# Moving the later SBUF buffers of a two-block transformer kernel up by 32 bytes, and one zero matmul more in nine groups of matmuls

## The chip, the cores and the metric

The kernel runs on one core of a Trainium2 chip, as one launch. The metric is the device time of that launch in microseconds (us). Below, TensorE is PE, its weight loads are PEld, VectorE is DVE, ScalarE is ACT, GpSimd is POOL, and SyncE is SP, which issues the loads of the weights.

## What is computed

Two transformer blocks of depth 1 run one after the other on x of 256 tokens by 2048 features, in float32. Each block is modulated by a vector c through one large matrix-vector product (`w_mod`, `w_ada_2`, 2048 to 12288).

```python
def first_block(x, c, ...):
    mod = (silu(c) @ w_mod + b_mod)                     # six vectors of 2048
    h = rmsnorm(x, mix_pre_w) * (1 + sc_m) + sh_m
    y = hybrid_mixer(h, w_in, ..., w_out)               # short convolution beside gated linear attention
    x = x + g_m * rmsnorm(y, mix_post_w)
    h = rmsnorm(x, ffn_pre_w) * (1 + sc_f) + sh_f
    y = conv_ffn(h, w_up, ffn_conv_w, w_down)           # 2048 -> 2 x 5632 -> 2048
    return x + g_f * rmsnorm(y, ffn_post_w)

def second_block(x, c, ...):
    mod = silu(c) @ w_ada + b_ada
    proj = (rms_norm(x, norm1_w) * (1 + scale1) + shift1) @ w_in
    u_pool, q, k, v, g_a, g_b = split(proj)
    y_a = multiscale_pool(u_pool, ...) @ w_a_up
    y_b = stick_breaking_attention(q, k, v) @ w_b_up
    x = x + gate1 * ((sigmoid(g_a) * y_a + sigmoid(g_b) * y_b) @ w_o)
    h2 = rms_norm(x, norm2_w) * (1 + scale2) + shift2
    return x + gate2 * (square(relu(h2 @ w_ff1)) @ w_ff2)
```

## The kernel before

Activations lie transposed: 128 features on the partitions, 256 tokens along the free dimension, 16 such tiles for 2048 features. To keep float32 precision, each number is split in two parts that TensorE takes: a rounded high part and the rest. `H`, `Y`, `FB`, `YAB`, `MG` and `FC` hold for each tile 512 columns, the high parts of 256 tokens and behind them their rests. A weight tile of 128 x 128 has its high part in `WH` and its rest in `WL`: ACT rounds `raw` into `WH`, DVE subtracts into `WL`.

A product of one weight tile with one activation tile is then, in `run_tile`, a **pair** of matmuls, one of 512 columns and one of 256:

```python
PE.matmul(bank(n)[:, :], wh, rhs, start=(kk == 0), stop=False)                # L585
return PE.matmul(bank(n)[:, T:2 * T], wl, rhs[:, 0:T], start=False, stop=ends) # L586
```

or, for jobs in `FOLDED`, three matmuls of 256 columns (L582 to L584). The moving operand is the activation tile, so it is read from `H` in the stages w_up, w_in_2 and w_ff1; from `FB` in w_down; from `YAB` in w_a_up_2 and w_b_up_2; from `MG` in w_o_2; from `FC` in w_ff2.

The order of work is written out by hand. `SLOTS` is a list of slots; a slot is mostly one load of weights, that is one job of 8 to 16 tiles (one output tile of 128 features). All engines walk it, each with its own lag, and semaphores tie them: PE waits for a weight unit (`s_lo`), for its bank to be emptied (`s_taken`), and in the first job of a group (`opens`) once per tile for the activation tile. The stages stand in this order: w_in with its sixteen parts, w_out, `AT_NORM1`, w_up and w_down in four groups (`FB`; the last group is folded), `AT_NORM2`, w_in_2, w_a_up_2, then two gates `ga` and `gb` from w_in_2 (`gb` alternates with w_b_up_2: 16 tiles from `H`, 8 from `YAB`), w_o_2, `AT_NORM3`, w_ff1 and w_ff2 in four groups (`FC`; the last two groups follow one another).

Here and there PE does other small products between the halves of a slot (`side`: gated linear attention, pooling, attention heads). At two places, `AT_NORM1 + 9` and `AT_NORM3 + 12`, it issues `beat`: a matmul of bf16 zeros, 512 columns, into `PS[1]` at a moment when it holds nothing (L621). `zeros` (L618) is the same for clearing.

SBUF tensors are laid out one behind the other in the order of the `sb` calls. `X`, `H`, `raw`, `WH`, `WL` and the constants come first, `eps` is the last of the constants, and behind it lie, one over another by stage, `raw2`, `Y`, `Q1` and so on, `FB`, `Y2`, `M`, `YAB`, `MG`, `FC`. As built, `H` is at byte 32896 of each partition (a multiple of 64) and `eps` at 152512. `raw2`, `Y`, `FB0`, `M` and `FC0` are at 152544, `YAB` at 168928, `FB1` at 175072, `FC1` at 185312, `MG` at 189408: each is 32 bytes past a multiple of 64. A tile of `H`, `FB`, `YAB`, `MG` or `FC` is 2048 bytes in each partition.

Of the kernel before, what the change touches and what calls it, by code (L numbers as in the profile page):

```python
# [109 lines left out]
LOADS, UNITS, UNITS_OF = [], [], []  # L110
# [57 lines left out]
SLOTS = [ls for ls in QKV]  # L168
# [9 lines left out]
AT_GB = len(SLOTS)  # L178
SLOTS += slots_of(L_GB) + [[]] * 2
SLOTS += slots_of(L_WO) + [[]]  # L180
AT_NORM3 = len(SLOTS)
# [75 lines left out]
MOD_COUNT = {STREAM[i][1:]: c + 1 for c, i in enumerate(MOD_ITEMS)}  # L257

SPLITS = [[] for _ in range(NSLOT)]
MODS_AT = [[] for _ in range(NSLOT)]
# [19 lines left out]
def build(nc, A, out):  # L282
    with ExitStack() as ctx:
        def sb(name, shape, dt=F32, on=ctx):
            return on.enter_context(nc.sbuf_tensor(name, shape, dt))

        def ps(name, shape):
            return ctx.enter_context(nc.psum_tensor(name, shape, F32))

        def sem(name):  # L290
            return ctx.enter_context(nc.semaphore(name))

        V, S, PE, G, SP = nc.vector, nc.scalar, nc.tensor, nc.gpsimd, nc.sync
# [15 lines left out]
        rstd = sb("rstd", [128, T])  # L309
        rstd2 = sb("rstd2", [128, T])  # L310
        SX = sb("SX", [128, T])
        eps = sb("eps", [128, 8])

        PM = [ps(f"PM{i}", [128, 512]) for i in range(NBANK)]
        PS = [ps(f"PS{i}", [128, 1024]) for i in range(2)]
# [80 lines left out]
        def load_aps(l, slot):  # L396
# [47 lines left out]
        s_yc, s_yr, s_f, s_ya, s_yb, s_mg, s_f2 = (  # L444
            sem(x) for x in ("s_yc", "s_yr", "s_f", "s_ya", "s_yb", "s_mg", "s_f2"))
# [92 lines left out]
        def tensor():  # L538
# [49 lines left out]
            def run(ls, which):  # L588
                for t in range(len(UNITS[UNITS_OF[ls[0]][which]])):
                    for l in ls:  # L590
                        u = UNITS_OF[l][which]
                        if t == 0:
                            PE.wait_ge(s_lo, u + 1)
                        n, kk = UNITS[u][t]
                        m = RANK if JOBS[n].kind == "alr" else 128
                        c = slice(t * m, (t + 1) * m)
                        mm = run_tile(n, kk, WH[:, u % NUNIT, c], WL[:, u % NUNIT, c])
                        if t == len(UNITS[u]) - 1:
                            mm.then_inc(s_unit, 1)

            def run_v(l, which):

                u = UNITS_OF[l][which]
                k = UNITS[u][0][1]
                PE.wait_ge(s_lo, u + 1)
                for half in range(2):
                    hi = H[:, k, half * 128:half * 128 + 128]
                    lo = H[:, k, T + half * 128:T + half * 128 + 128]
                    for c in range(2):
                        b = slice(c * 512, (c + 1) * 512)  # L610
                        PE.matmul(PS[half][:, b], hi, WH[:, u % NUNIT, b], start=(k == 0), stop=False)  # L611
                        PE.matmul(PS[half][:, b], hi, WL[:, u % NUNIT, b], start=False, stop=False)  # L612
                        mm = PE.matmul(PS[half][:, b], lo, WH[:, u % NUNIT, b], start=False, stop=(k == 15))  # L613
                mm.then_inc(s_unit, 1)
# [5 lines left out]
            def beat(b):  # L620
                PE.matmul(b, zero.broadcast_to([128, 128]), zero.broadcast_to([128, 512]), start=True, stop=True)  # L621

            def clear(half, again):

                for c in range(2):
                    zeros(PS[half][:, c * 512:(c + 1) * 512])
                for _ in range(again):
                    zeros(PS[half][:, 512:1024], start=False)
# [17 lines left out]
            def y_sums(use):  # L646

                PE.wait_ge(s_yadd, 15 * (use + 1))
                PE.matmul(S0, mean[:, :], ST[use][:, 0, :], start=True, stop=False)
                PE.wait_ge(s_ysq, 16 * (use + 1))  # L650
                PE.matmul(S0, mean[:, :], SQ[use][:, 1, 0, :], start=False, stop=True).then_inc(s_ysum, 1)
                PE.matmul(S23, mean[:, :], ST[use][:, 1:3, :].rearrange("p q t -> p (q t)"), start=True, stop=False)
                PE.wait_ge(s_yz, 16 * (use + 1))
                PE.wait_ge(s_xz, 16 * (use + 1))
                PE.matmul(S23, mean[:, :], SQ[use][:, 1, 1:3, :].rearrange("p q t -> p (q t)"), start=False,
                          stop=True).then_inc(s_ysum, 1)

            def x_sums():
                PE.wait_ge(s_yadd, 45)
                PE.matmul(S0, mean[:, :], gt[:, 2, :], start=True, stop=False)  # L660
                PE.wait_ge(s_ysq, 48)
                PE.matmul(S0, mean[:, :], gt[:, 1, :], start=False, stop=True).then_inc(s_ysum, 1)
# [122 lines left out]
            def side(s, half):  # L785
                if AT_ALR <= s < AT_NORM1:
                    gla(2 * (s - AT_ALR + 7) + half)
                elif AT_NORM2 <= s < AT_GB:
                    heads(2 * (s - AT_NORM2 - 1) + half)

            start_up()
            for s, ls in enumerate(SLOTS):
                if s == AT_NORM1:
                    PE.wait_ge(s_gact, ACT_RSTD)
                    y_sums(0)
                    clear(1, 8)
                    PE.wait_ge(s_u, 1)
                    clear(0, 8)
                elif s == AT_NORM2:
                    PE.wait_ge(s_o, 2)  # L800
                    y_sums(1)
                    clear(1, 8)
                    PE.wait_ge(s_u, 2)
                    clear(0, 8)
                elif s == AT_NORM3:
                    PE.wait_ge(s_hdve, 11 + 6 * 3 + 2)
                    x_sums()
                    clear(1, 8)
                    PE.wait_ge(s_rstd, 6)
                    clear(0, 2)  # L810

                if s == AT_NORM1 + 9:
                    PE.wait_ge(s_o, 2)
                    beat(PS[1][:, 0:512])
                elif s == AT_NORM3 + 12:
                    PE.wait_ge(s_gh, 2)
                    for c in range(2):
                        beat(PS[1][:, c * 512:(c + 1) * 512])
                for n in DONE[s]:
                    if USE_OF[n]:  # L820
                        PE.wait_ge(s_taken[BANK_OF[n]], USE_OF[n])
                    else:
                        PE.wait_ge(s_at, BANK_OF[n] + 1)
                if s < AT_ALR:
                    for which in range(2):
                        run(ls[0:1], which)
                        run_v(ls[1], which)
                elif ls and ls[0] in L_V2:
                    if ls[0] == L_V2[0]:
                        PE.wait_ge(s_ya, 8)  # L830
                        PE.wait_ge(s_hact, 11)
                    run_v(ls[0], 0)
                    side(s, 0)
                    run_v(ls[0], 1)
                elif ls:
                    if ls[0] == L_AUP[0]:
                        PE.wait_ge(s_hact, 15)
                    run(ls, 0)
                    side(s, 0)
                    if len(UNITS_OF[ls[0]]) > 1:  # L840
                        run(ls, 1)
                side(s, 1)
# [913 lines left out]
        N_ALR = JOB_OF["alr", 0, 48]  # L1756

        tensor()
        scalar()
        vector()  # L1760
# [70 lines left out]
```

## Time and profile before

| | |
|---|---|
| time, median of 3 runs | 2525.01 us (2524.55 to 2526.55) |
| the profiled execution, its own time | 2522.16 us |
| its span | 2520.8 us |
| mean granted TensorE clock | 0.997 of full speed |
| PE busy / DVE busy / ACT busy | 2464.6 / 2001.0 / 1289.1 us |

The span is from the first to the last instruction. The profiled execution is one run, 2.85 us below the median of the three timed ones. Matmuls are pipelined and overlap in the record (a matmul of 512 columns is shown as 0.39 us long although the next starts 0.23 us later), so the pace of PE is read from the starts of successive matmuls and not from their durations.

### The profile page before, as it was taken

Reading aid. Unit: us, or ns where it says so; the run is one execution under the profiler, and the core shown is the slowest. Engines: PE = TensorE matmul, PEld = TensorE weight load, DVE = VectorE, ACT = ScalarE, POOL = GpSimd, SP = SyncE. Lnnn points to the kernel's source line nnn. Section 1 sums busy time; section 2 is a strip of 40 time slices with the busy share of each in tenths; the row PEclk is TensorE's granted clock in tenths of the full one; section 3 lists DMA queues with packets and bytes.
Section 4 is the critical chain, followed back from the end, with each engine's and each line's share of the span. In section 5 each row is a group of like instructions: output and inputs, shape, how many; then the busy total and the mean of one; then the engine's idle time right before and its main releaser. Section 6 shows DMA issues by size and latency. Waiting matters only on the chain.

```text
span 2520.8 us, 38361 instructions
## 1 busy us (share of the span) xinstructions
PE 2464.6 (98%) x15321; PEld 2203.0 (87%) x15321; DVE 2001.0 (79%) x2640; ACT 1289.1 (51%) x1883; POOL 4.0 (0%) x11
## 2 busy tenths in 40 slices
PE   6799999999999999999999999999999999999999
PEld 5689999898888888889888888888898888888888
DVE  7879998978977888889968688998678756556555
ACT  5454455555654555555546566554454444444443
POOL 0000000000000000000000000000000000000000
PEclk9999999999999999999999999999999999999999
DMA  9988898667777778778558677888578755555553
GB/s 374 391 306 315 327 356 298 238 223 271 266 256 263 259 250 291 260 258 267 180 190 331 232 281 261 321 316 293 184 259 316 259 184 189 194 185 188 193 188 134
DMA packets 142387, 652.16 MB, mean 259 GB/s; under 512 B 13009, under 2 KB 64209, under 8 KB 77441
## 3 DMA queue, kind: packets, MB, share of 16 engines
q1 hardware_dynamic: 141106, 645.06, 71.6%
q0 software_dynamic: 672, 3.31, 0.3%
q8 instruction: 121, 1.98, 0.3%
q10 hardware_dynamic: 432, 1.35, 0.2%
q14 instruction: 56, 0.46, 0.1%
HBM read 647.58 MB, written 2.10 MB: 258 GB/s over the span
## 4 chain that ended last, share of the span: by engine, by line
PE 82%; DVE 9%; DMA 4%; issue 2%; ACT 2%; DVEq 0%; SPq 0%; ACTq 0%
PE PM L585 45%; PE PM L586 23%; DVE WL L1224 3%; DVE raw L1231 3%; DMA raw<-in_w_in 3%; PE PM L582 2%; PE PM L583 2%; PE PM L584 2%; PE PS L582 2%; PE PS L583 2%; PE PS L584 2%; PE PS L611 1%; PE PS L612 1%; PE PS L613 1%; DMA raw<-in_w_mod 0%
## 5 line engine op out<-in xcount | busy, mean ns | idle before, releaser
L858 ACT CAST WH<-raw 128x1024 fp32r<-128x1024 f32 (+1 forms) x881 | 880.8, 1011 | 985.7 <-PE PM L586 658.7
L1224 DVE TENSOR_TENSOR WL<-raw,WH 128x1024 fp32r<-128x1024 f32 (+1 forms) x881 | 1016.6, 1172 | 419.0 <-ACT WH L858 416.4
L585 PE MATMUL PM<-H,WH 128*128 128x512 f32 x2944 | 1027.3, 393 | 0.0
L586 PE MATMUL PM<-H,WL 128*128 128x256 f32 x2944 | 823.1, 280 | 0.0
L585 PEld LDWEIGHTS PM<-H,WH 128*128 128x128 f32 x2944 | 551.3, 187 | 124.9 <-issue 0.4
L586 PEld LDWEIGHTS PM<-H,WL 128*128 128x128 f32 x2944 | 555.7, 189 | 0.1
L1231 DVE CUSTOM_DVE_ANT_0 raw<-raw,cb 128x2048 f32<-128x2048 f32 x192 | 437.0, 2284 | 1.7 <-DMA raw<-in_w_mod 1.2
L585 PE MATMUL PM<-FC,WH 128*128 128x512 f32 x1024 | 358.7, 393 | 0.0
L586 PE MATMUL PM<-FC,WL 128*128 128x256 f32 x1024 | 285.8, 279 | 0.0
L585 PEld LDWEIGHTS PM<-FC,WH 128*128 128x128 f32 x1024 | 191.9, 187 | 45.7
L582 PE MATMUL PM<-H,WH 128*128 128x256 f32 (+1 forms) x656 | 192.2, 293 | 35.7 <-DVE H L1255 29.8
L586 PEld LDWEIGHTS PM<-FC,WL 128*128 128x128 f32 x1024 | 191.9, 187 | 0.0
L584 PE MATMUL PM<-H,WL 128*128 128x256 f32 (+1 forms) x656 | 189.7, 289 | 0.0
L583 PE MATMUL PM<-H,WH 128*128 128x256 f32 (+1 forms) x656 | 189.6, 289 | 0.0
L585 PE MATMUL PM<-FB,WH 128*128 128x512 f32 x528 | 185.0, 393 | 0.0
L582 PEld LDWEIGHTS PM<-H,WH 128*128 128x128 f32 (+1 forms) x656 | 128.2, 195 | 43.0 <-DVE WL L1224 34.0
L586 PE MATMUL PM<-FB,WL 128*128 128x256 f32 x528 | 147.4, 279 | 0.0
L864 ACT COPY tmps<-PM 128x256 f32<-128x256 f32 x328 | 118.9, 363 | 54.1 <-PE PM L586 54.0
L583 PEld LDWEIGHTS PM<-H,WH 128*128 128x128 f32 (+1 forms) x656 | 128.3, 196 | 0.6
L584 PEld LDWEIGHTS PM<-H,WL 128*128 128x128 f32 (+1 forms) x656 | 128.4, 196 | 0.4
L585 PEld LDWEIGHTS PM<-FB,WH 128*128 128x128 f32 x528 | 98.9, 187 | 23.7
L582 PE MATMUL PS<-H,WH 128*128 128x256 f32 x384 | 108.9, 284 | 4.2 <-DVE H L1258 4.2
(329 smaller groups left out, 3125.2 us busy)
## 6 DMA issues: line engine op xcount, KB each, us to landing
raw<-in_w_ff SPq DMA_DIRECT2D x128, 1024.0 KB, 4.9
raw<-in_w_in SPq DMA_DIRECT2D x112, 1024.0 KB, 6.3
raw<-in_w_mod SPq DMA_DIRECT2D x96, 1024.0 KB, 7.1
raw<-in_w_ada SPq DMA_DIRECT2D x96, 1024.0 KB, 6.1
raw<-in_w_up SPq DMA_DIRECT2D x80, 1024.0 KB, 5.2
raw<-in_w_down SPq DMA_DIRECT2D x64, 704.0 KB, 5.2
raw<-in_w_out SPq DMA_DIRECT2D x16, 1024.0 KB, 6.6
raw<-in_w_o SPq DMA_DIRECT2D x16, 1024.0 KB, 6.2
```

Source lines behind the costliest of these rows:

```text
L582: PE.matmul(acc(n), wh, rhs[:, 0:T], start=(kk == 0 and not beside), stop=False)
L583: PE.matmul(acc(n), wh, rhs[:, T:2 * T], start=False, stop=False)
L584: return PE.matmul(acc(n), wl, rhs[:, 0:T], start=False, stop=ends)
L585: PE.matmul(bank(n)[:, :], wh, rhs, start=(kk == 0), stop=False)
L586: return PE.matmul(bank(n)[:, T:2 * T], wl, rhs[:, 0:T], start=False, stop=ends)
L611: PE.matmul(PS[half][:, b], hi, WH[:, u % NUNIT, b], start=(k == 0), stop=False)
L612: PE.matmul(PS[half][:, b], hi, WL[:, u % NUNIT, b], start=False, stop=False)
L613: mm = PE.matmul(PS[half][:, b], lo, WH[:, u % NUNIT, b], start=False, stop=(k == 15))
L858: S.copy(part(WH), w).then_inc(s_hi, 1)
L864: S.copy(low(n), bank(n)[:, T:2 * T]).then_inc(s_low, 1)
L1224: V.tensor_tensor(part(WL), w, part(WH).bitcast(F32), ALU.subtract).then_inc(s_lo, 1)
L1231: V.tensor_tensor_reduce(w, w, cb[:, :], 1.0, 0.0, ALU.mult, ALU.add, mods[:, which, tile:tile + 1]).then_inc(s_mod, 1)
```

## The change

`eps` gets 16 columns where it had 8, so that everything behind it lies 32 bytes higher: `raw2`, `Y`, `FB0`, `M` and `FC0` at 152576, `YAB` at 168960, `FB1` at 175104, `FC1` at 185344, `MG` at 189440, all multiples of 64. `ug`, `uv` and `exact` were at multiples of 64 and are now 32 bytes past one. And PE issues one more `beat` at the start of nine slots: the slot behind the first one of each group of w_down (four), of w_ff2 (four) and of w_o_2 (one).

```diff
+BEAT_AT = [s + 1 for s, ls in enumerate(SLOTS) if ls and LOADS[ls[0]][0] in ("w_down", "w_ff2_2", "w_o_2")
+           and LOADS[ls[0]][-1] == 0]
...
-        eps = sb("eps", [128, 8])
+        eps = sb("eps", [128, 16])
...
                 if s == AT_NORM1 + 9:
                     PE.wait_ge(s_o, 2)
                     beat(PS[1][:, 0:512])
                 elif s == AT_NORM3 + 12:
                     PE.wait_ge(s_gh, 2)
                     for c in range(2):
                         beat(PS[1][:, c * 512:(c + 1) * 512])
+                elif s in BEAT_AT:
+                    if AT_GB < s < AT_NORM3:
+                        PE.wait_ge(s_yb, 8)
+                    beat(PS[1][:, 0:512])
```

On PE, at the border between the first and the second job of the first group of w_ff2, stand before (FC0 is the moving operand, WH and WL the two parts of the weights, PM1 and PM2 the banks of the two jobs):

```order
L585 MATMUL PM1<-FC0,WH 128x512 [waits s_f2]
L586 MATMUL PM1<-FC0,WL 128x256
L585 MATMUL PM2<-FC0,WH 128x512 [waits s_lo,s_taken2]
L586 MATMUL PM2<-FC0,WL 128x256
L585 MATMUL PM2<-FC0,WH 128x512
```

and with the change (four lines were added above, so L585 is L589):

```order
L589 MATMUL PM1<-FC0,WH 128x512 [waits s_f2]
L590 MATMUL PM1<-FC0,WL 128x256
L625 MATMUL PS1<-eps 128x512
L589 MATMUL PM2<-FC0,WH 128x512 [waits s_lo,s_taken2]
L590 MATMUL PM2<-FC0,WL 128x256
```

One matmul of 512 columns without a wait of its own now stands between the two jobs; nothing else moved. The same border in w_o_2 (MG is the moving operand) reads with the change:

```order
L589 MATMUL PM1<-MG,WH 128x512 [waits s_mg]
L590 MATMUL PM1<-MG,WL 128x256
L625 MATMUL PS1<-eps 128x512 [waits s_yb]
L589 MATMUL PM2<-MG,WH 128x512 [waits s_lo,s_taken2]
L590 MATMUL PM2<-MG,WL 128x256
```

Here the added matmul waits for `s_yb`, which DVE raises when it has written the last tile of `YAB`. The other engines have the same instructions in the same order as before.

## Rows read from the trace of the kernel before

**Rows 1.** The page: span, TensorE, and the chain that ended last, by engine.

```profile
span 2520.8 us, 38361 instructions
PE 2464.6 (98%) x15321; PEld 2203.0 (87%) x15321; DVE 2001.0 (79%) x2640; ACT 1289.1 (51%) x1883; POOL 4.0 (0%) x11
PE 82%; DVE 9%; DMA 4%; issue 2%; ACT 2%; DVEq 0%; SPq 0%; ACTq 0%
```

**Rows 2.** Chain from 700 to 800 us, by line; then PE's longest wait overall.

```profile
by line: PE PM L585 66.4%; PE PM L586 33.7%
...
PE PM L582 <- DVE H L1255: 29.8, 12, 6.7
```

**Rows 3.** Groups of PE by line: busy us, mean ns | idle us before.

```profile
L585 PE MATMUL PM<-FC,WH 128*128 128x512 f32 x1024 | 358.7, 393 | 0.0
...
L585 PE MATMUL PM<-FB,WH 128*128 128x512 f32 x528 | 185.0, 393 | 0.0
...
L585 PE MATMUL PM<-YAB,WH 128*128 128x512 f32 x256 | 91.5, 397 | 0.5 <-DVE WL L1224 0.5
L585 PE MATMUL PM<-MG,WH 128*128 128x512 f32 x224 | 78.4, 393 | 0.0
```

**Rows 4.** Timeline of PE (start us, us, what): borders around w_ff2's first group.

```profile
1981.47 0.40 PE L585 MATMUL PM<-FC,WH 128*128 128x512 f32 x1
...
2071.12 0.40 PE L585 MATMUL PM<-H,WH 128*128 128x512 f32 x1
...
2159.87 0.40 PE L585 MATMUL PM<-FC,WH 128*128 128x512 f32 x1
```

**Rows 5.** Timeline of PE: start and end of w_down's first group.

```profile
724.36 0.39 PE L585 MATMUL PM<-FB,WH 128*128 128x512 f32 x1
...
785.97 0.40 PE L585 MATMUL PM<-H,WH 128*128 128x512 f32 x1
```

**Rows 6.** Timeline of PE: start of w_o_2, start of its folded jobs.

```profile
1705.40 0.39 PE L585 MATMUL PM<-MG,WH 128*128 128x512 f32 x1
...
1783.80 0.28 PE L582 MATMUL PM<-MG,WH 128*128 128x256 f32 x1
```

**Rows 7.** Line 585 from 2338.3 us on: count, ns min/median/max, first and last start.

```profile
L585 PE MATMUL PM<-FC,WH x511: 389/394/422, 2338.3 to 2516.8; 128*128 128x512 f32 x171
```

**Rows 8.** Timeline of PE around the beat at `AT_NORM1 + 9`.

```profile
529.64 0.40 PE L585 MATMUL PM<-H,WH 128*128 128x512 f32 x1
529.88 0.28 PE L586 MATMUL PM<-H,WL 128*128 128x256 f32 x1
530.00 0.39 PE L621 MATMUL PS<-eps 128*128 128x512 bf16 x1
530.04 0.58 PE L585 MATMUL PM<-H,WH 128*128 128x512 f32 x1
...
530.57 0.40 PE L585 MATMUL PM<-H,WH 128*128 128x512 f32 x1
```

**Rows 9.** Timeline of PE before the two beats at `AT_NORM3 + 12`.

```profile
1861.60 0.40 PE L585 MATMUL PM<-H,WH 128*128 128x512 f32 x1
...
1861.96 0.40 PE L585 MATMUL PM<-H,WH 128*128 128x512 f32 x1
...
1862.31 0.40 PE L585 MATMUL PM<-H,WH 128*128 128x512 f32 x1
...
1862.66 0.40 PE L585 MATMUL PM<-H,WH 128*128 128x512 f32 x1
```

**Rows 10.** Timeline of PE: end of the gates ga; one round of gb and w_b_up_2.

```profile
1575.18 0.40 PE L585 MATMUL PM<-H,WH 128*128 128x512 f32 x1
...
1576.24 0.40 PE L585 MATMUL PM<-H,WH 128*128 128x512 f32 x1
...
1604.60 0.40 PE L585 MATMUL PM<-H,WH 128*128 128x512 f32 x1
...
1613.00 0.40 PE L585 MATMUL PM<-H,WH 128*128 128x512 f32 x1
```

**Rows 11.** Folded jobs: weight loads of line 582, from `H` and from `FB`.

```profile
L582 PEld LDWEIGHTS PS<-H,WH x128: 186/192/192, 1801.3 to 1847.0; 128*128 128x128 f32 x128
...
L582 PEld LDWEIGHTS PM<-FB,WH x173: 187/187/187, 1153.9 to 1215.9; 128*128 128x128 f32 x173
```

**Rows 12.** Line 1542, which raises `s_yb`.

```profile
L1542 DVE TENSOR_TENSOR YAB<-PS,YAB x8: 414/420/425, 1476.3 to 1565.7; 128x256 fp32r<-128x256 f32 x8
```

## The prediction, made before the changed kernel had run

> **What bounds the kernel now.** I read the page first: PE is busy 98% of the span, DVE 79%, and 82% of the chain that ended last is PE's [rows 1]. Busy time says little for matmuls that overlap, so I asked what the chain holds inside the feed-forward part: nothing but L585 and L586 [rows 2]. PE's longest total wait, 29.8 us for DVE's `H`, belongs to the folded jobs of the openings and of w_in (L582), and the large groups that the change touches show no idle time of PE before them worth naming: 0.0, 0.0, 0.5 and 0.0 us [rows 3]. So there a nanosecond of pace is a nanosecond of time, and nothing hides a matmul that is added. Then I took the pace from the starts in the timeline. The reader is to see that one and the same pair of matmuls has three paces:
>
> - from `H`, w_ff1 between the groups of w_ff2: 256 pairs from 2071.12 to 2159.87 us, 346.7 ns each [rows 4];
> - from `FC`, `FB` and `MG`: 256 pairs in 89.65 us, 176 in 61.61, 224 in 78.40, and 510 from 2338.3 to 2516.8, each time 350.0 to 350.2 ns [rows 4 to 7];
> - from `H` again, but uneven: starts 360, 350 and 350 ns apart, three pairs in 1.06 us, 353.3 ns on average [rows 9], and so at the end of the gates ga, 1.06 us from 1575.18 to 1576.24 [rows 10].
>
> I call them the even, the offset and the uneven pace. The granted clock averages 0.997 of full speed, 2.4 GHz, over the whole span, so it is not that. The weights, shapes and banks are the same; the offset pace has the buffers that lie 32 bytes past a multiple of 64, and never `H`. 3.3 ns is 8 columns of a 512-column matmul at 2.4 GHz (8 / 2.4), and 32 bytes are 8 numbers of float32. If TensorE reads a row of the moving operand in pieces of 64 bytes, a shifted row costs it one piece more, half of it useless at either end. That is an inference from these rows, and a good fit.
>
> **The change part by part.** *The 32 bytes.* Pairs from shifted buffers number 1024 + 528 + 256 + 224 = 2032 [rows 3]. At the even pace the stretches shrink so:
>
> - `FC`: the first two groups 89.65 - 88.75 = 0.90 us each, borders included [rows 4]; the last 512 pairs 512 x 3.3 ns = 1.7 us [rows 7]. Together 3.5.
> - `FB`: 61.61 - 176 x 0.3467 = 0.59 us for each of three groups [rows 5], 1.8.
> - `MG`: 78.40 - 224 x 0.3467 = 0.74 us [rows 6].
>
> That is -6.0 us. The folded jobs give nothing: three matmuls take 45.7 / 127 = 360 ns from `H` and 62.0 / 172 = 360 ns from `FB` [rows 11], so a limit other than the read of the moving operand (the weight loads, three of them instead of two) covers the shift there, and `Y` and the folded part of `FB` and `MG` stay as they are. What DVE and ACT do with shifted tiles is off the path. `ug`, `uv` and `exact` get the shift instead; `exact` is only a weight of some small products, and I take nothing for them.
>
> *The beats.* The one at `AT_NORM1 + 9` lies between a pair that starts at 529.64 and a pair that starts at 530.57: 0.93 us for two pairs and the beat, so the beat is 0.93 - 2 x 0.347 = 0.24 us [rows 8] (with uneven pairs in place of even, 0.22). Nine of them are +2.2 us, all on the path. None waits: two carry no wait but PE's own place in line, and that of w_o_2 waits for `s_yb`, raised last at 1565.7 us, 140 us earlier [rows 12, 6]. ACT and DVE wait for PE at these borders, not PE for them, so 0.24 us more lets nothing run late.
>
> *What the beats do.* Before the two older ones the pace was uneven [rows 9] and behind them it is even: from 1871 us on `H` keeps to it, as the stretch from 2071.12 on shows [rows 4]. So a beat sets the even pace. It can only give that back where the pace would be uneven, 6.6 ns a pair.
>
> *Where the new layout ends up uneven.* This is the part that I cannot read off directly. Until now each passage through a shifted buffer seems to have ended in the even pace: ga ends uneven at 1576.24, then the first eight pairs from `YAB` come, and the rounds of gb and w_b_up_2 take 8.40 us for 24 pairs [rows 10], where 16 even and 8 offset pairs would be 8.35. With `YAB` aligned nothing is left in these rounds that I know to end the uneven pace, and the next beat is in w_o_2. From 1576.6 to 1705.4 there are 368 pairs. Uneven they take 368 x 353.3 = 130.0 us against 128.8 now, +1.2 us; even, 127.6, -1.2 us. The 128 pairs of w_a_up_2 from `YAB` stand between attention products and go from 350.0 to 353.3 or 346.7, +0.4 or -0.4. I take the uneven one for both, as ga is uneven in most of its stretches and ends so.
>
> The sum: -6.0 + 2.2 + 1.2 + 0.4 = -2.2 us. The profiled execution goes from 2522.16 to about 2520.0, and as the median of the timed runs stands 2.85 us above it, the median from 2525.0 to 2522.8.
>
> By a rule of the Trainium skill the gain should not be there at all: its page "SBUF — State Buffer" says, in the box on cachelines under "Door 1: The DMA port swizzle", that SBUF has lines of 16 bytes, and crossing to a new line is what costs. A start that is 32 bytes past a multiple of 64 is still at the start of such a line. The 3.3 ns of rows 4 to 7 speak against that for the 512-column read, unless something else sets `FC`, `FB` and `MG` apart from `H`; the rival is priced below.
>
> **The rivals.**
>
> 1. *Even pace everywhere.* The uneven pace dies out before gb, or ga itself becomes even as w_a_up_2 before it changes. -6.0 + 2.2 - 1.2 - 0.4 = -5.4 us, 2519.6. For it: PE leaves the uneven pace after some of the attention products already. Against: ga runs uneven up to its last pair. If also 200 pairs of ga turn even, -1.3 more, 2518.3.
> 2. *The shift is not the cause.* Then it is the place in SBUF, or what is written there meanwhile; the pace of 350 ns stays and the beats are a pure cost: +2.2 us, 2527.2. Against: four buffers at four places, with different writers, have the one pace of 350.0, and `MG` lies at the place of other tensors. (The 16-byte rule of the Trainium skill's page "SBUF — State Buffer" is this rival.)
> 3. *The beat upsets an even stream.* Both places where beats stand now had the uneven pace ahead of them [rows 9]; none shows what a beat does to an even one. If it turned it uneven, the 1679 pairs behind the nine beats in their groups would be at 353.3 (+5.6 us against now), the 1216 pairs from `H` that follow between the groups too (+8.1), and with the beats, 2.2, and w_b_up_2 and w_a_up_2, 1.6, the kernel would be slower by 17.5 us, 2542. The sign turns to slower by 0.2% once some 1330 pairs are uneven that I hold to be even (5.05 + 3.8 us at 6.6 ns). Against: the beat's short weight load and its 512 columns give the next weight load time, whatever the pace before.
> 4. *The first job of a group is the cause.* Its sixteen waits may by themselves break the even pace once the buffers are aligned; then the beats earn their place, and the loss is only one job of each group, 16 x 6.6 ns, under 0.1 us each, 0.7 in all. It does not change the sign.
>
> **How the numbers follow.** A measurement of this kernel can tell about 0.2% (5.05 us) from no change. Chances: the forecast with its variant 4, 0.42; rival 1, 0.34 (even everywhere 0.24, with ga 0.10); rival 2, 0.12; rival 3, 0.06; something that I don't see, such as a pace of the attention products that the shift of `exact` and of `Q2`, `K2`, `AT` changes, 0.06. Rival 1 lies just beyond the limit of 0.2%, so I count two thirds of its plain form and all of its variant as faster: 0.16 + 0.10, with 0.02 of the unseen, 0.28. Slower is rival 3 and some of the unseen, 0.08. The rest, 0.64, is within 0.2%. The range reaches from rival 1 with part of ga, 2518.6, to rival 2, 2527.3; what it leaves out is rival 3, the far side of rival 1 and the unseen.
>
> **What would show it.** In the profile of the changed kernel the groups of 256 pairs from `FC` should take 88.75 + 0.24 us and those from `FB` 61.02 + 0.24; nine more rows of the beat's line, each followed by a pair 0.93 us later; the rounds of gb 8.48 us if uneven and 8.32 if even; the folded stages unchanged at 360 ns. If `FC` still shows 350 ns, rival 2 holds and my cause is wrong. If starts of 360, 350 and 350 ns appear behind the new beats, it is rival 3. If the rounds of gb take 8.32 us, the forecast is 3 us too high. A wait of PE for `s_yb` or a DMA that PE waits for in these groups would break the argument that nothing else moves.

## The result

| | before | with the change |
|---|---|---|
| time, median | 2524.49 us (2521.69 to 2526.55, 10 runs) | 2532.07 us (2529.46 to 2535.57, 10 runs) |
| ratio, 95% interval | | 1.0032 (1.0025 to 1.004) |
| the profiled execution, its own time / span | 2522.16 / 2520.8 us | 2529.46 / 2528.1 us |
| mean granted TensorE clock | 0.997 | 0.996 |

The changed kernel is slower by 7.6 us, where the prediction had it faster by 2.2, and lies above its range (2518.6 to 2527.3 us). The page of the changed kernel, first lines and the chain by line:

```profile
span 2528.1 us, 38365 instructions
...
PE 2474.5 (98%) x15316; PEld 2206.4 (87%) x15330; DVE 2001.4 (79%) x2640; ACT 1289.7 (51%) x1883; POOL 4.0 (0%) x11
...
PE 83%; DVE 11%; issue 2%; DMA 2%; ACT 2%; DVEq 0%; SPq 0%; ACTq 0%
PE PM L589 45%; PE PM L590 23%; DVE raw L1239 4%; DVE WL L1232 4%; PE PM L586 2%; PE PM L588 2%; PE PM L587 2%; PE PS L586 2%; PE PS L588 2%; PE PS L587 2%; DMA raw<-in_w_in 1%; DMA raw<-in_w_mod 1%; PE PS L615 1%; PE PS L617 1%; PE PS L616 1%
```

The bound is the same: PE on the chain, no new wait. Its pace changed. The timeline of PE with the change (start us, us, what), at the borders that [rows 4], [rows 5] and [rows 6] show for before:

```profile
718.94 0.39 PE L589 MATMUL PM<-FB,WH 128*128 128x512 f32 x1
...
780.96 0.39 PE L589 MATMUL PM<-H,WH 128*128 128x512 f32 x1
...
905.32 0.39 PE L589 MATMUL PM<-FB,WH 128*128 128x512 f32 x1
...
1706.95 0.40 PE L589 MATMUL PM<-MG,WH 128*128 128x512 f32 x1
...
1785.81 0.28 PE L586 MATMUL PM<-MG,WH 128*128 128x256 f32 x1
...
1983.50 0.39 PE L589 MATMUL PM<-FC,WH 128*128 128x512 f32 x1
...
1984.54 0.40 PE L589 MATMUL PM<-FC,WH 128*128 128x512 f32 x1
...
1984.89 0.39 PE L589 MATMUL PM<-FC,WH 128*128 128x512 f32 x1
...
1985.24 0.39 PE L589 MATMUL PM<-FC,WH 128*128 128x512 f32 x1
...
2073.60 0.39 PE L589 MATMUL PM<-H,WH 128*128 128x512 f32 x1
...
2075.35 0.40 PE L589 MATMUL PM<-H,WH 128*128 128x512 f32 x1
...
2075.71 0.40 PE L589 MATMUL PM<-H,WH 128*128 128x512 f32 x1
...
2076.06 0.40 PE L589 MATMUL PM<-H,WH 128*128 128x512 f32 x1
...
2076.41 0.40 PE L589 MATMUL PM<-H,WH 128*128 128x512 f32 x1
...
2164.04 0.39 PE L589 MATMUL PM<-FC,WH 128*128 128x512 f32 x1
```

The first group from `FC` takes 90.10 us where it took 89.65, the first from `FB` 62.02 where it took 61.61, `MG` 78.86 for 78.40. More is lost behind them: 256 pairs from `H`, a buffer that did not move, take 90.44 us where they took 88.75, and 352 pairs from `H` between the groups of w_down 124.36 where they took 122.04. The rows inside the two stretches say how. The first three pairs from `FC` run at 346.7 ns (1983.50 to 1984.54), the next two 350 ns apart, long before the group's new beat, which stands behind 16 pairs; the group settles at starts 354, 346 and 353 ns apart, 351.1 on average. The `H` behind it (2075.35 to 2076.41) has starts 360, 350 and 350 ns apart: the uneven pace, where before it was even. Stage by stage against before:

| stretch | pairs | us against before |
|---|---|---|
| `FB`, three groups, with a beat each | 528 | +1.2 |
| `H` between them | 704 | +4.6 |
| gb with w_b_up_2, then `MG`, with a beat | 592 | +1.4 |
| `FC`, four groups, with a beat each | 1024 | +1.9 |
| `H` between them | 512 | +3.4 |
| up to the start of `FB` (718.94 against 724.36) | | -5.4 |

(By the starts and ends of the stretches in both timelines; the last `FC` one is 179.9 for 178.9 us.) That is 12.5 us lost and 5.4 won, 7.1 of the 7.3 us between the spans. The 5.4 us stand in no term of the prediction either. By 138 us DVE is already 4.5 us ahead of before, and up to there the chain of before is mostly DMA (`raw` from `w_in` alone is 49% of it). DMA traffic from 30 to 100 us, with the change:

```profile
DMA packets 12794, 28.07 MB, mean 401 GB/s; under 512 B 427, under 2 KB 10648, under 8 KB 10648
```

The kernel before moved 390 GB/s there.

### The profile page after: what moved, and what is told of

Same layout as the page of the kernel before. It is cut to its first block, busy times and chain, and to the rows that moved or that the text cites. A ratio compares the mean times of both kernels' runs of the same rounds, so it can differ in the third digit from the quotient of the medians.

```text
span 2528.1 us, 38365 instructions
## 1 busy us (share of the span) xinstructions
PE 2474.5 (98%) x15316; PEld 2206.4 (87%) x15330; DVE 2001.4 (79%) x2640; ACT 1289.7 (51%) x1883; POOL 4.0 (0%) x11
## 4 chain that ended last, share of the span: by engine, by line
PE 83%; DVE 11%; issue 2%; DMA 2%; ACT 2%; DVEq 0%; SPq 0%; ACTq 0%
PE PM L589 45%; PE PM L590 23%; DVE raw L1239 4%; DVE WL L1232 4%; PE PM L586 2%; PE PM L588 2%; PE PM L587 2%; PE PS L586 2%; PE PS L588 2%; PE PS L587 2%; DMA raw<-in_w_in 1%; DMA raw<-in_w_mod 1%; PE PS L615 1%; PE PS L617 1%; PE PS L616 1%
## 5 line engine op out<-in xcount | busy, mean ns | idle before, releaser
L589 PE MATMUL PM<-H,WH 128*128 128x512 f32 x2944 | 1036.8, 397 | 0.0
L589 PEld LDWEIGHTS PM<-H,WH 128*128 128x128 f32 x2944 | 552.7, 188 | 133.5 <-issue 0.2
L589 PE MATMUL PM<-FC,WH 128*128 128x512 f32 x1024 | 360.6, 394 | 0.0
L589 PEld LDWEIGHTS PM<-FC,WH 128*128 128x128 f32 x1024 | 192.4, 188 | 44.3
L589 PE MATMUL PM<-FB,WH 128*128 128x512 f32 x528 | 186.2, 395 | 0.0
L589 PEld LDWEIGHTS PM<-FB,WH 128*128 128x128 f32 x528 | 99.2, 188 | 22.8
```

## Experiments

What moves in them is the place of four things within 256 bytes: `H` (and `raw`, which lies whole tiles behind it), `WH`, `WL`, and the later buffers (`raw2`, `FB`, `YAB`, `MG`, `FC`). Paces are the mean distance between the starts of pairs; the two columns on the right are those of w_ff2 and w_ff1. "One run" is one profiled execution with its time; runs of before range over 7 us, so the verdicts there rest on the stretches.

| kernel | `H` | `WH` | `WL` | later | pairs from `FC`, ns | from `H` behind `FC`, ns |
|---|---|---|---|---|---|---|
| before, and beats alone | 128 | 128 | 128 | 224 | 350.0 | 346.7 |
| the change, and 32 bytes alone | 128 | 128 | 128 | 0 | 351.1 | 353.3 |
| later at 128 | 128 | 128 | 128 | 128 | 346.7 | 346.7 |
| later at 64 | 128 | 128 | 128 | 64 | 353.3 | 353.3 |
| later at 192 | 128 | 128 | 128 | 192 | 353.3 | 346.7 |
| weights moved | 128 | 0 | 0 | 0 | 353.3 | 351.1 |
| only `WL` moved | 128 | 128 | 0 | 128 | 350.0 | 350.0 |
| all at 0 | 0 | 0 | 0 | 0 | 346.7 | 346.7 |

Two rows hide something. Later at 128 has 353.3 ns in all of w_down, from `FB` and from `H`, at the same places that give 346.7 in the table. And with the weights moved, `FC` lies at the place of the weights and runs at 353.3.

### The 32 bytes alone

```diff
-        eps = sb("eps", [128, 8])
+        eps = sb("eps", [128, 16])
```

> Only the 32 bytes, no new beat. Theory W (the waits of a group's first job break the even pace of an aligned buffer, and once broken it stays uneven into the H stretch behind the group): FC and FB at about 351 ns a pair, H between the groups at 353.3 ns, span 2526 us, that is the changed kernel less nine beats of 0.24 us; ratio to before 1.002 to 1.003. Theory B (the added beat upsets an even stream): without it FC, FB and H are all at 346.7 ns, median near 2520 us, ratio 0.998.

2531.0 us (11 runs) against 2525.01; ratio 1.0023 (1.0014 to 1.0032). Its timeline at the same borders:

```profile
719.49 0.39 PE L585 MATMUL PM<-FB,WH 128*128 128x512 f32 x1
...
781.28 0.40 PE L585 MATMUL PM<-H,WH 128*128 128x512 f32 x1
...
905.65 0.39 PE L585 MATMUL PM<-FB,WH 128*128 128x512 f32 x1
```

`FB` takes 61.79 us and `H` behind it 124.37. With no new beat anywhere, `H` is uneven behind every shifted buffer. So the loss of pace belongs to the 32 bytes: 5.1 us in the stretches of w_down, 1.2 from gb to the end of `MG`, 4.4 from the first `FC` on, 10.7 in all against before, of which 4.9 come back before the first `FB`.

### The nine beats alone

The change without the wider `eps`.

> Only the nine beats, buffers 32 bytes past a multiple of 64 as before. Theory W: offset pace of 350.0 ns behind each beat, H even at 346.7 ns between the groups, + 9 x 0.24 = 2.2 us, ratio 1.0009. Theory B: H is uneven (353.3 ns) behind the groups, 1216 pairs x 6.6 ns = 8 us more, ratio 1.004.

2525.15 us (11 runs) against 2525.01; ratio 1.0007 (0.9998 to 1.0016). In the timeline:

```profile
1983.29 0.40 PE L589 MATMUL PM<-FC,WH 128*128 128x512 f32 x1
...
2073.17 0.39 PE L589 MATMUL PM<-H,WH 128*128 128x512 f32 x1
...
2161.91 0.40 PE L589 MATMUL PM<-FC,WH 128*128 128x512 f32 x1
```

89.88 us for `FC`, 0.23 more than before, and 88.74 for `H`, the same. By these stretches a beat costs what it was priced at, 0.23 us, and upsets nothing here. The timed runs by themselves can't tell the nine beats from nothing.

### Beats in the middle of even stretches

```diff
+MID_H = [s for s, ls in enumerate(SLOTS) if ls and LOADS[ls[0]] in (("w_up", 12), ("w_up", 28), ("w_up", 38), ("w_ff1_2", 20), ("w_ff1_2", 40), ("w_ff1_2", 56))]
...
+                elif s in MID_H:
+                    beat(PS[1][:, 0:512])
```

> The kernel before with six beats in the middle of even stretches from H (three in w_up, three in w_ff1), none at the groups' starts. Theory W: each costs 0.24 us and the pace behind it is 346.7 ns as ahead of it; 1.4 us in all. Theory B: 353.3 ns behind each, until the next group from FB or FC starts; some 176 pairs each in w_up and 128 in w_ff1, about 6 us in all.

One run, 2528.5 us, layout of before. The three in w_up and the first in w_ff1 leave `H` at 346.7 ns. The second in w_ff1 does not:

```profile
2119.41 0.39 PE L586 MATMUL PM<-H,WH 128*128 128x512 f32 x1
2119.64 0.28 PE L587 MATMUL PM<-H,WL 128*128 128x256 f32 x1
2119.76 0.39 PE L622 MATMUL PS<-eps 128*128 128x512 bf16 x1
2119.80 0.58 PE L586 MATMUL PM<-H,WH 128*128 128x512 f32 x1
```

Behind it `H` is at 353.3 ns up to the next `FC`, and behind the third again. A beat is no setter of the even pace: it shakes the stream, which then settles either way.

### The later buffers at the place of `H`

```diff
-        eps = sb("eps", [128, 8])
+        eps = sb("eps", [128, 48])
```

> No new beat, eps with 48 columns, so that FB, FC, MG and YAB start at 128 modulo 256 bytes as H does (after the 32-byte change they start at 0 modulo 256). If the place modulo 256 sets the pace: FC and FB at 346.7 ns and H even between, span near 2515 us. Theory W, for which only multiples of 64 count: the same paces as with 16 columns, 351 and 353.3 ns.

```profile
729.32 0.40 PE L585 MATMUL PM<-FB,WH 128*128 128x512 f32 x1
...
791.51 0.40 PE L585 MATMUL PM<-H,WH 128*128 128x512 f32 x1
...
1995.70 0.39 PE L585 MATMUL PM<-FC,WH 128*128 128x512 f32 x1
...
2084.45 0.39 PE L585 MATMUL PM<-H,WH 128*128 128x512 f32 x1
```

One run, 2532.83 us. `FC` takes 88.75 us, the figure that I had forecast for the change, with the same waits in its first job; so the waits are not what breaks the pace in the change, the place is. But here the one beat at `AT_NORM1 + 9` left `H` uneven, and `FB`, at the same place, has nothing that ends it: 62.19 us, 353.3 ns, through all of w_down. The even and the uneven pace are both lasting states when everything lies at one place. So the same place allows 346.7 ns and does not secure it: this kernel, with every operand at one place, was no faster than the change.

### Multiples of 64 that are not that place

`eps` with 32 columns puts the later buffers at 64, with 64 columns at 192.

> eps with 32 columns, no new beat: FC, FB, MG, YAB at 64 modulo 256 bytes, the weights WH and WL and H at 128. If the pace goes by the start modulo 128: as at 0 modulo 256, that is no even pace, about 351 ns, and H behind it uneven (353.3); here 64 is not 0 modulo 128, so another pattern. If only the place that H has (128 modulo 256) can hold the even pace: not 346.7 ns in FC. If any multiple of 64 but 0 can: 346.7 ns in w_ff2.

> eps with 64 columns, no new beat: the later buffers at 192 modulo 256. Same question. If what counts is the place modulo 128, this is as e5 (64 modulo 128).

One run each, 2536.64 and 2529.77 us. The timeline with the later buffers at 64:

```profile
1989.36 0.39 PE L585 MATMUL PM<-FC,WH 128*128 128x512 f32 x1
...
2079.80 0.39 PE L585 MATMUL PM<-H,WH 128*128 128x512 f32 x1
...
2170.25 0.39 PE L585 MATMUL PM<-FC,WH 128*128 128x512 f32 x1
```

90.44 us for 256 pairs, 353.3 ns, and 90.45 for `H` behind them. At 192 two patterns appear: 353.3 ns in `FC` and in the second and third group of `FB`, with an even `H` behind, and 348.9 ns in the first group of `FB`, with an uneven `H` behind, and in `MG`. Both places are multiples of 64, so that being one is worth nothing by itself.

### The weights moved instead

128 bytes between `raw` and `WH`, and `eps` widened to keep the later buffers at 0.

```diff
+        sb("pad", [128, 32])
...
-        eps = sb("eps", [128, 8])
+        eps = sb("eps", [128, 48])
```

> 128 bytes put ahead of WH: WH and WL at 0 modulo 256, H at 128, and the later buffers at 0. If the place of the moving operand relative to that of the weights counts: H now shows the pattern that FC had at 0 (351 ns), and FC can be even (346.7 ns) or uneven (353.3). If only the moving operand's own place counts: as the kernel with the 32 bytes alone, FC 351.1, H 346.7 or 353.3 ns.

One run, 2536.91 us. `H` has not moved, yet it now has the pace that `FC` has in the change:

```profile
2081.14 0.39 PE L586 MATMUL PM<-H,WH 128*128 128x512 f32 x1
...
2171.03 0.40 PE L586 MATMUL PM<-FC,WH 128*128 128x512 f32 x1
...
2261.48 0.39 PE L586 MATMUL PM<-H,WH 128*128 128x512 f32 x1
```

89.89 us for 256 pairs, 351.1 ns, with starts 354, 346 and 353 ns apart. `H` is here 128 bytes from the weights' place, as `FC` was in the change. `FC`, now at the weights' place, takes 90.45 us (2171.03 to 2261.48), 353.3 ns: one of the two paces expected there, and the slow one. What counts is the place of the moving operand relative to that of the weights.

### Everything at one place, a multiple of 256

128 bytes ahead of `H`, and `eps` widened.

```diff
+        sb("pad", [128, 32])
...
-        eps = sb("eps", [128, 8])
+        eps = sb("eps", [128, 48])
```

> 128 bytes put ahead of H: H, WH, WL and the later buffers all at 0 modulo 256. If the relative place counts: only 346.7 and 353.3 ns in all stages. If the moving operand's own place counts: 351.1 ns also from H.

> The kernel with H, WH, WL and the later buffers all at one place modulo 256, timed. Theory R (the place of the moving operand relative to the weights sets which paces there are; at the same place they are even, 346.7, and uneven, 353.3, and either lasts until something ends it): FC, FB follow H's pace; 2512 to 2520 us, by whether the single beat at AT_NORM1 + 9 ends in the even pace. Theory M (the one run at 2512 us was a fast front and luck): within 0.2% of before.

The one run of the first was 2512.45 us. Timed: 2514.96 us (5 runs) against 2524.34; ratio 0.9964 (0.9952 to 0.9976). Faster than both kernels. The timeline of the timed one:

```profile
718.84 0.39 PE L586 MATMUL PM<-FB,WH 128*128 128x512 f32 x1
...
779.85 0.39 PE L586 MATMUL PM<-H,WH 128*128 128x512 f32 x1
...
901.88 0.39 PE L586 MATMUL PM<-FB,WH 128*128 128x512 f32 x1
...
1976.68 0.39 PE L586 MATMUL PM<-FC,WH 128*128 128x512 f32 x1
...
2065.42 0.39 PE L586 MATMUL PM<-H,WH 128*128 128x512 f32 x1
```

`FB` 61.01 us, `H` 122.03, `FC` 88.74: all at 346.7 ns. gb and `MG` stayed uneven, which takes 2.0 us back. The spans differ by 8.4 us: 5.4 won in `FB` and `FC` (by the differences of their starts), 2.0 and 0.6 lost in the uneven stretches, and 5.5 won before the first pair, for which see the loads below.

### Beats on top of that layout

> As e10, with two beats in place of one at AT_NORM1 + 9 and two at AT_GB + 2. Theory R with lasting paces: gb, w_b_up_2 and w_o_2 turn even, 346.7 ns, some 570 pairs x 6.6 = 3.8 us less, 0.7 us for three beats more: ratio to before 0.994 to 0.996 and below e10's. If beats have no say there, 0.7 us more than e10.

> As e10, with the nine beats of the change. Rival 3 of the prediction (a beat upsets an even stream) would give stretches at 353.3 ns behind some of the nine, up to 8 us; if beats leave an even stream even, nine times 0.24 us more than e10, less 208 pairs x 6.6 ns = 1.4 us where the beat of w_o_2 ends the uneven pace: ratio to before 0.995 to 0.997.

The first has two beats at `AT_NORM1 + 9` and two at `AT_GB + 2`, to end the uneven pace of gb: 2514.44 us (9 runs), ratio 0.996 (0.9947 to 0.9973), no gain over the layout alone. In its trace the end of ga was already even, and the two beats (1572.82 us) turned it uneven, 353.3 ns up to the end of `MG`. The second has the nine beats of the change: 2516.62 us (5 runs), ratio 0.997 (0.9958 to 0.9981). Its timeline at the third group of w_down:

```profile
1095.61 0.39 PE L626 MATMUL PS<-eps 128*128 128x512 bf16 x1
1095.65 0.58 PE L590 MATMUL PM<-FB,WH 128*128 128x512 f32 x1
```

Ahead of it 346.7 ns, behind it 353.3 for the rest of the group. The one of w_o_2 did the reverse: `MG` went from 353.3 to 346.7. The other seven changed no pace.

### Only `WL` moved

128 bytes between `WH` and `WL`; the later buffers come to 128.

```diff
+        sb("pad", [128, 32])
...
-        eps = sb("eps", [128, 8])
+        eps = sb("eps", [128, 16])
```

> 128 bytes ahead of WL alone: H, WH and all later buffers at 128 modulo 256, WL at 0; no new beat. If it is the place of the high weights WH relative to the moving operand that counts: 346.7 or 353.3 ns from H and FC alike. If it is that of WL: 351.1 ns from both. If both count: something else from both, neither 351.1 nor 346.7 ns.

```profile
1978.55 0.40 PE L586 MATMUL PM<-FC,WH 128*128 128x512 f32 x1
...
2068.15 0.40 PE L586 MATMUL PM<-H,WH 128*128 128x512 f32 x1
```

One run, 2520.79 us. `H` and `FC` behave alike, as they lie at one place, and know two paces, 346.7 and 350.0 ns; 353.3 never occurs in a long stretch. So the place of `WL` counts too, and with it elsewhere the disturbed pace costs half as much (3.3 ns a pair in place of 6.6).

### The loads, read across all traces

No kernel was made for the 5.4 us; the fourteen traces hold the test. The rows of DMA traffic from 30 to 100 us of the beats alone, of later at 128, of the weights moved and of all at 0:

```profile
DMA packets 12524, 27.31 MB, mean 390 GB/s; under 512 B 418, under 2 KB 10446, under 8 KB 10446
```

```profile
DMA packets 12535, 27.31 MB, mean 390 GB/s; under 512 B 420, under 2 KB 10458, under 8 KB 10458
```

```profile
DMA packets 12784, 28.08 MB, mean 401 GB/s; under 512 B 425, under 2 KB 10636, under 8 KB 10636
```

```profile
DMA packets 12758, 28.63 MB, mean 409 GB/s; under 512 B 432, under 2 KB 10529, under 8 KB 10529
```

| `raw` / `raw2`, place in 256 bytes | traces | GB/s, 30 to 100 us | median landing of a `w_mod` load, 0 to 150 us | first pair of w_up |
|---|---|---|---|---|
| 128 / 224, 128, 64 or 192 | 7 | 390 | 11.7 or 11.8 us | 524.3 to 528.1 us |
| 128 / 0 | 3 | 401 | 10.9 to 11.2 us | 518.9, 519.5, 524.3 us |
| 0 / 0 | 4 | 409 to 411 | 10.3 to 10.8 us | 517.9, 518.8, 519.5, 525.2 us |

The first 48 loads, issued by 131 us, go by turns to four slots of `raw` and four of `raw2`. With none of them at a multiple of 256 they move 390 GB/s, with half 401, with all about 410. The places are 0 or 256 within 512 bytes in the fast ones, so it is 256 that counts. By 138 us VectorE is 4.1 to 4.5 us ahead of before in the three kernels of the second row of the table and 6.1 to 6.6 ahead in the four of the third. Two of the seven, the weights moved and the nine beats at one place, lose 3.3 and 5.4 us of it again between 340 and 380 us. The granted clock from 350 to 400 us averages 0.97 and 0.93 there and 1.00 in the other five, which may be why. Four kernels of the first row have 0.97 there too, and lose 1.8 to 2.6 us.

The packets themselves show it. From 30 to 100 us before has 10002 packets of 1024 bytes and 2077 of 8192. A packet of 1024 bytes takes 50.8 ns on average; with the change, where half of the landing places are at a multiple of 256, it takes 48.6, and with all at 0 46.1. The median of those of 8192 bytes is 313 ns before and 309 in both others.

The Trainium skill has the rule, in its page "DMA: Bandwidth & Descriptors", section "How a descriptor splits into AXI transactions": a transaction must start at a multiple of 256 bytes, and a long transfer is split into transactions of 256. The page tells it of the bytes that are fetched; what moved here is where they land. An estimate from its rule: a row of 8192 bytes that starts elsewhere has 33 transactions in place of 32, 3% more, and one of 1024 bytes 5 in place of 4, 25% more. The traces agree in direction, and in that the short rows lose more, but each loses less than the estimate: 50.8 against 46.1 ns is 10%, 313 against 309 is 1%, and 409 against 390 GB/s over all loads of that stretch is 5%.

## Why the prediction was wrong

**The step that failed** is "The 32 bytes: at the even pace the stretches shrink", -6.0 us. By 32 bytes alone the pairs from `FC`, `FB` and `MG` measure +1.8 us: 351.1 ns where I had 346.7. The step rested on the inference that TensorE reads the moving row in pieces of 64 bytes. "A good fit" was a fit of one difference between two places, `H` and 32 bytes past a multiple of 64, which many periods fit. Later at 64 and at 192 refute it: multiples of 64, and 353.3 or 348.9 ns. What the runs showed in its place is a dependence on the distance to the weights modulo 256: 0 apart, 346.7 or 353.3; 96 apart, as before, 350.0; 128 apart, as the change puts it, 351.1. The change moved the buffers from one distance that isn't 0 to another, and the new one is the worse.

**What I left out behind it** was the larger part. I held `H` to stay even, as the shifted buffers had always handed it over so in the trace of before. At 128 apart they hand it over uneven: 1216 pairs from `H` at 353.3 ns, 8.0 of the 10.7 us. Rival 3 names just this stretch and its price of 8.1 us, but blames the beats; the run with 32 bytes alone has the same stretches uneven without them.

**The beats' price** was right: 0.23 to 0.24 us each in the stretches of the beats alone, some 2.2 in all. "None waits" held too. **"A beat sets the even pace"** was half right: it follows from one kind of place, a beat in an uneven stream. In an even one it may do nothing (most of them) or turn it uneven (w_ff1 with the beats in even stretches, w_down with nine beats at one place); and one left an uneven stream uneven (later at 128).

**Where the new layout ends up uneven** came nearly as forecast for the rounds of gb and w_b_up_2: 8.46 us each where I had 8.48, and +0.9 us in all where I had +1.2. `H` is uneven there; the pairs from `YAB` are not, they stay at 350 to 351 ns. So do those of w_a_up_2, and its +0.4 did not come.

**The rivals.** The even pace everywhere did not come. That the shift is not the cause is refuted by 32 bytes alone; the 16-byte rule of the Trainium skill's page "SBUF — State Buffer" ("Door 1: The DMA port swizzle") would have all these kernels run at one pace, as all places are multiples of 16, and their pairs take from 346.7 to 353.3 ns. That the first job's waits break the pace is refuted by later at 128, where the same waits leave it even. Two sums of rival 3 are off, and neither bears on the result: the pairs behind the nine beats are 1663 (3 x 165, 208 and 4 x 240), not 1679, and the sign would turn at some 1100 uneven pairs (5.05 + 2.2 us at 6.6 ns), not 1330, as the 1.6 us of w_b_up_2 and w_a_up_2 were already in the forecast. And eight of the nine beats carry no wait, not two.

**A term that was missing with the other sign:** the section on the change lists `raw2` among the buffers that move, from 224 to 0 within 256 bytes, and I read only what TensorE reads. As a landing place for DMA it is worth about 5 us. The medians agree: 12.5 - 5.4 = 7.1 us, 7.6 measured. Had I seen this alone, I would have forecast a faster kernel yet.

**What stays open** is the mechanism in TensorE: why the two operands' places interact, why `WL` counts with `WH`, and what decides which way a beat or a border turns the stream. The even pace has two forms, starts 347, 346, 347 ns and 350, 343, 350 ns apart, so a phase between loads and matmuls may be part of it. That is not shown. It is open, too, how firmly a layout leads to its pace: each kernel has one trace, though those of like layout agree in their paces from `FC`. The period could be 512 as well as 256 for the matmuls.

## What to carry to other kernels

Put the rows on which weights are loaded at multiples of 256 bytes: here that is worth some 5 us before the first pair of w_up. Putting the moving operand and the weights at the same place modulo 256 allows the fastest pace but does not secure it: all at 0 took 9.4 us less than 2524, by both effects, while later at 128, with the operands at one place too, took 2532.83 us in its one run. So read the starts in the trace of the kernel that you mean to keep. When buffers shift, list everything that reads or writes each of them, DMA included, and test an alignment idea against more than two places before it is given a term. On a PE-bound stream a small disturbance can change the pace of hundreds of matmuls behind it, so price what follows an edit and not only the edit.

## What the runs showed of the hardware

- A pair of a 512- and a 256-column matmul in rounded float32 has at least five paces at one granted clock: 346.7, 348.9, 350.0, 351.1 and 353.3 ns. Which of them it has goes by the places of the operands and by what went before.
- With all operands at one place the streams of 346.7 and of 353.3 ns both last for a thousand pairs (w_ff1 and w_ff2 of all at 0; w_down of later at 128).
- A matmul of zeros, 0.24 us, switched such a stream in both directions.
- Loads into SBUF rows that start at a multiple of 256 bytes moved 409 to 411 GB/s, others 390; a packet of 1024 bytes took 46.1 ns in the first case and 50.8 in the second.
